# Opening of a one-core two-block transformer kernel: who issues the norm row and the first input transfer, and when the input's quarters are turned and squared

## The reference, cut to what matters

```python
def rms_norm(x, w):
    xf = x.astype(jnp.float32)
    y = xf * lax.rsqrt(jnp.mean(xf * xf, axis=-1, keepdims=True) + EPS)
    return (y * w.astype(jnp.float32)).astype(x.dtype)
...
def mixer_block(u, w_in, lb, hg_norm_w, rel_bias, w_branch_a, w_branch_b, w_out):
    z = u @ w_in
    ...
    return merged @ w_out
...
    h = x
    h = h + mixer_block(rms_norm(h, norm_mix_w[l]), w_in[l], ...)
    u = rms_norm(h, norm_mlp_w[l])
    h = h + jnp.square(jax.nn.relu(u @ w_up[l])) @ w_down[l]
```

## Time and profile before

| what | before |
|---|---|
| median of 3 runs | 1920.42 us (1920.09 to 1922.02) |
| profiled execution, its own time | 1919.19 us |
| its span | 1917.4 us |
| TensorE matmul, busy | 1889.7 us, 99% of the span |
| TensorE weight load, busy | 1752.5 us, 91% |
| VectorE, busy | 1101.7 us, 57% |
| ScalarE, busy | 914.2 us, 48% |
| GpSimd, busy | 178.9 us, 9% |
| mean traffic of the DMA engines | 181 GB/s |

### The profile page before, as it was taken

One profiled execution on the slowest core, in us unless ns is written; L12 is line 12 of the kernel. 1 busy time (PEld: TensorE's weight loads), 2 busy tenths in 40 slices (PEclk: granted clock), 3 DMA queues, 4 the chain that ended last, 5 costly groups with the idle time before them and its releaser, 6 DMA issues.

```text
span 1917.4 us, 33984 instructions
## 1 busy us (share of the span) xinstructions
PE 1889.7 (99%) x13468; PEld 1752.5 (91%) x13468; DVE 1101.7 (57%) x1265; ACT 914.2 (48%) x1189; POOL 178.9 (9%) x135
## 2 busy tenths in 40 slices
PE   9999999999999999999999999999999999998998
PEld 9989998999999889988998899899889998888986
DVE  6655766466655555554545545554566457766664
ACT  6534444565644455443443344344454354655543
POOL 2001331401000100000010000000010000031000
PEclk9999999999999999999999999999999999999999
DMA  8665656566565656666656666566555554444454
GB/s 272 191 180 171 185 179 177 152 193 177 171 220 186 208 187 177 196 199 189 196 187 198 190 195 194 190 183 202 188 185 173 175 170 133 116 136 144 133 187 143
DMA packets 176435, 346.49 MB, mean 181 GB/s; under 512 B 10976, under 2 KB 11184, under 8 KB 175776
## 3 DMA queue, kind: packets, MB, share of 16 engines
q1 hardware_dynamic: 174176, 337.76, 57.0%
q0 software_dynamic: 2128, 6.82, 1.4%
HBM read 342.44 MB, written 2.10 MB: 180 GB/s over the span
## 4 chain that ended last, share of the span: by engine, by line
PE 94%; DVE 3%; ACT 2%; issue 1%; DMA 0%; SPq 0%; POOL 0%; DVEq 0%; ACTq 0%
PE ps L430 56%; PE ps L442 32%; DVE wlo L1240 1%; ACT whi L857 1%; PE ps L758 1%; PE ps L527 1%; PE ps L745 1%; PE ps L722 0%; PE ps L460 0%; DMA x_nat<-in_x_dram 0%; PE ps L733 0%; PE ps L578 0%; PE ps L696 0%; DVE p L1652 0%; PE ps L570 0%
## 5 line engine op out<-in xcount | busy, mean ns | idle before, releaser
L1240 DVE TENSOR_TENSOR wlo<-raw,whi 128x1024 fp32r<-128x1024 f32 x631 | 804.1, 1280 | 719.3 <-ACT whi L857 718.3
L857 ACT ACTIVATE whi<-raw 128x1024 fp32r<-128x1024 f32 x631 | 664.1, 1058 | 872.6 <-PE ps L430 545.1
L430 PE MATMUL ps<-xhi,whi 128*128 128x256 f32 (+1 forms) x1984 | 567.3, 286 | 0.0
L430 PE MATMUL ps<-xhi,wlo 128*128 128x256 f32 (+1 forms) x1984 | 555.4, 280 | 0.0
L430 PE MATMUL ps<-xlo,whi 128*128 128x256 f32 (+1 forms) x1952 | 546.8, 280 | 0.0
L430 PEld LDWEIGHTS ps<-xhi,whi 128*128 128x128 f32 x1984 | 375.0, 189 | 10.0 <-issue 7.6
L430 PEld LDWEIGHTS ps<-xhi,wlo 128*128 128x128 f32 x1984 | 373.8, 188 | 0.0
L430 PEld LDWEIGHTS ps<-xlo,whi 128*128 128x128 f32 x1952 | 368.8, 189 | 1.5 <-issue 0.7
L430 PE MATMUL ps<-x2hi,whi 128*128 128x256 f32 x1024 | 282.8, 276 | 0.0
L430 PE MATMUL ps<-x2lo,whi 128*128 128x256 f32 x1024 | 282.7, 276 | 0.0
L430 PE MATMUL ps<-x2hi,wlo 128*128 128x256 f32 x1024 | 282.7, 276 | 0.0
(11 more groups left out here) (357 smaller groups left out, 2220.6 us busy)
## 6 DMA issues: line engine op xcount, KB each, us to landing
raw<-in_w_in_dram SPq DMA_DIRECT2D x279, 512.0 KB, 3.8
raw<-in_w_up_dram SPq DMA_DIRECT2D x128, 512.0 KB, 3.8
raw<-in_w_down_dram SPq DMA_DIRECT2D x128, 512.0 KB, 3.7
raw<-in_w_out_dram SPq DMA_DIRECT2D x64, 512.0 KB, 4.0
raw<-in_w_branch_a_dram SPq DMA_DIRECT2D x16, 512.0 KB, 4.2
raw<-in_w_branch_b_dram SPq DMA_DIRECT2D x16, 512.0 KB, 4.1
x_nat<-in_x_dram SPq DMA_DIRECT2D x4, 512.0 KB, 7.0
rel<-in_rel_turned_dram POOLq DMA_DIRECT2D x8, 256.0 KB, 4.4
```

The source lines that it names most:

```text
L430: ins = mm(outs[b], w[:, k % SLOTS, j, cols], v, start=start, stop=last and j == CK - 1 and i == 2, skip_group_check=True)
L857: f(whi[:, k % SLOTS], raw[:, k % SLOTS], ACT.Copy).then_inc(whi_ready, 1)
L1240: tt(wlo[:, k % SLOTS], raw[:, k % SLOTS], whi[:, k % SLOTS], ALU.subtract).then_inc(wlo_ready, 1)
```

## The change

- ScalarE issues the identity and `mix_rows`, ahead of its first table load; SyncE starts with the input at once.
- Quarter 0 of the input comes in two half transfers of 256 columns, the first (`x_first`) ahead of chunk 0's halves and the second (`x_in[0]`) behind them. Of chunks 1 to 3 and quarters 1 to 3 the chunk is issued first.
- TensorE waits for `x_first`, and within quarter 0 for `x_in[0]` ahead of row tile 2. Quarter c (1 to 3) is turned directly before chunk c, so one chunk later than before.
- The squares of quarter k are taken behind chunk 4 + k, by ScalarE and VectorE. The sum moves from behind chunk 4 to behind chunk 8, the square root from behind chunk 5 to behind chunk 8, reciprocal and `diag_m` from behind chunk 5 to behind chunk 9, the copy of `row_m` from behind chunk 10 to behind chunk 11.
- `row_scale()` stands before chunk 7 instead of chunk 6.

```diff
--- before.py
+++ after.py
@@ -244,6 +244,7 @@
         set_free = [sem(f"set_free{i}") for i in range(2)]
         kvb_free = [sem("kvb_free0"), sem("kvb_free1")]
         x_in = [sem(f"x_in{c}") for c in range(4)]
+        x_first = sem("x_first")
         half_in, half_hi, half_lo = [sem(n) for n in ("half_in", "half_hi", "half_lo")]
         ident_in, c_in, meta_in = [sem(n) for n in ("ident_in", "c_in", "meta_in")]
         vec_in, vec_t, vec_ready = sem("vec_in"), sem("vec_t"), sem("vec_ready")
@@ -358,17 +359,17 @@
             def rows(w, k, cols):
                 return w[:, CK * k:CK * k + CK, cols]
 
-            sp.dma_start(ident[:], identity).then_inc(ident_in, 16)
-            sp.dma_start(mix_rows[:], norm_mix_w[0].rearrange("(k p) -> k p", p=P)).then_inc(mix_in, 16)
-            for c in range(4):
-                cols = slice(c * CW, (c + 1) * CW)
-                sp.dma_start(x_nat[:, :, cols], x[0, :, cols].rearrange("(t p) d -> p t d", p=P)).then_inc(x_in[c], 16)
-                if c == 0:
-                    first = rows(w_in_t, 0, slice(0, CW))
-                    sp.dma_start(raw[:, 0, 0], first[:, 0]).then_inc(half_in, 16)
-                    sp.dma_start(raw[:, 0, 1], first[:, 1]).then_inc(raw_in[0], 16)
-                else:
-                    chunk(C_IN, c, rows(w_in_t, c, slice(0, CW)))
+            def x_cols(lo, hi):
+                return x_nat[:, :, lo:hi], x[0, :, lo:hi].rearrange("(t p) d -> p t d", p=P)
+
+            first = rows(w_in_t, 0, slice(0, CW))
+            sp.dma_start(*x_cols(0, CW // 2)).then_inc(x_first, 16)
+            sp.dma_start(raw[:, 0, 0], first[:, 0]).then_inc(half_in, 16)
+            sp.dma_start(raw[:, 0, 1], first[:, 1]).then_inc(raw_in[0], 16)
+            sp.dma_start(*x_cols(CW // 2, CW)).then_inc(x_in[0], 16)
+            for c in range(1, 4):
+                chunk(C_IN, c, rows(w_in_t, c, slice(0, CW)))
+                sp.dma_start(*x_cols(c * CW, (c + 1) * CW)).then_inc(x_in[c], 16)
             for k in range(4, NC):
                 chunk(C_IN, k, rows(w_in_t, k, slice(0, CW)))
             with sp.Fori(1, G_IN) as g:
@@ -464,10 +465,12 @@
 
             def turn_start(c):
 
-                pe.wait_ge(x_in[c], 16)
+                pe.wait_ge(x_in[c] if c else x_first, 16)
                 if c >= 2:
                     pe.wait_ge(x_ready, 4 * c - 4)
                 for kt in range(4 * c, 4 * c + 4):
+                    if kt == 2:
+                        pe.wait_ge(x_in[0], 16)
                     for t in range(NT):
                         o = (kt % 2) * T + t * P
                         ins = nc.tensor.transpose(ps[:, 4 + (kt % 8) // 2, o:o + P],
@@ -605,11 +608,11 @@
                             warm(11)
                             turn_start(0)
                             warm(9)
-                        if k < 3:
-                            turn_start(k + 1)
+                        if 1 <= k < 4:
+                            turn_start(k)
                         if k == 3:
                             turn_vectors()
-                        if k == 6:
+                        if k == 7:
                             row_scale()
                         pe.wait_ge(x_ready, CK * (k + 1))
                     if natural:
@@ -878,10 +881,14 @@
                 f(uhi[:, kt, :], ps[:, 4 + (kt % 8) // 2, (kt % 2) * T:(kt % 2) * T + T], ACT.Copy,
                   scale=mix_w[:, kt:kt + 1]).then_inc(n_hi, 1)
 
+            act.dma_start(ident[:], identity).then_inc(ident_in, 16)
+            act.dma_start(mix_rows[:], norm_mix_w[0].rearrange("(k p) -> k p", p=P)).then_inc(mix_in, 16)
             act.wait_ge(setup, 1)
             f(ss[:, 14:15], eps_t[:], ACT.Sqrt)
             def start_squares(c):
 
+                if c == 0:
+                    act.wait_ge(x_first, 16)
                 act.wait_ge(x_in[c], 16)
                 cols = slice(c * CW, (c + 1) * CW)
                 square(0, c, x_nat[:, 0, cols], junk[:, cols], 0, n_ss)
@@ -896,10 +903,8 @@
                         f(whi[:, 0, j], raw[:, 0, j], ACT.Copy).then_inc((half_hi, whi_ready)[j], 1)
                 else:
                     split_hi(C_IN, k)
-                    start_squares(k - 1)
             for kt in range(12, KT):
                 start_upper(kt)
-            start_squares(3)
 
             def start_meta():
                 act.wait_ge(meta_in, 16)
@@ -988,7 +993,9 @@
             for g in range(G_IN):
                 for k in range(NC):
                     split_hi(C_IN + NC * g, LEAD + k)
-                    if g == 0 and k == 1:
+                    if g == 0 and k < 4:
+                        start_squares(k)
+                    if g == 0 and k == 4:
                         act.wait_ge(n_sum, 1)
                         f(ss[:, 0:2], ss[:, 0:2], ACT.Sqrt, bias=eps_t[:], scale=1.0 / D).then_inc(n_sd, 1)
                     if g == 0 and k == 5:
@@ -1258,6 +1265,8 @@
             own(nc.vector.memset(ones[:], 1.0))
             def start_squares(c):
 
+                if c == 0:
+                    dve.wait_ge(x_first, 16)
                 dve.wait_ge(x_in[c], 16)
                 cols = slice(c * CW, (c + 1) * CW)
                 nc.vector.tensor_tensor_reduce(junk_b[:, cols], x_nat[:, 1, cols], x_nat[:, 1, cols], 1.0, 0.0,
@@ -1275,17 +1284,17 @@
                         tt(wlo[:, 0, j], raw[:, 0, j], whi[:, 0, j], ALU.subtract).then_inc((half_lo, wlo_ready)[j], 1)
                 else:
                     split_lo(C_IN, k)
-                    start_squares(k - 1)
             for kt in range(12, KT):
                 start_lower(kt)
-            start_squares(3)
 
             def start_rows(k):
 
-                if k == 0:
+                if k < 4:
+                    start_squares(k)
+                if k == 4:
                     dve.wait_ge(n_ss, 8)
                     nc.vector.tensor_reduce(ss[:, 0:2], sq[:, 0], AX.X, ALU.add).then_inc(n_sum, 1)
-                if k == 1:
+                if k == 5:
                     dve.wait_ge(n_sd, 1)
                     nc.vector.reciprocal(rstd[:, 0:2], ss[:, 0:2]).then_inc(n_rs, 1)
                     dve.wait_ge(n_rs, 1)
```

## The result

| | before | after |
|---|---|---|
| median of 20 runs each | 1919.36 us (1917.02 to 1923.62) | 1923.94 us (1921.53 to 1925.95) |
| ratio after / before | | 1.0020, 95% interval 1.0013 to 1.0027 |
| profiled execution's span | 1917.4 us | 1920.9 us |
| start of chunk 0 | 10.23 | 10.80 |
| start of chunk 4 | 23.70 | 25.58 |

The change makes the kernel slower, by some 4.6 us between the medians and by 2.5 to 5.2 us by the interval. The median lies in the range given and near the forecast of 1923.2, partly by luck: with 20 runs the kernel before came out at 1919.36 instead of 1920.42, so the rise is 4.6 us where I had summed up 2.8. Two misses offset each other: chunk 0, forecast 0.6 us earlier, came 0.57 later, and the kernel before was itself 1.1 us faster than I had taken it.

A forecast was written before the change was run, and what follows sets the result against it. TensorE was taken to bound the kernel (94% of the span), so its standstills in the first 40 us count. Terms -0.6 + 0.8 + 0.7 + 1.85 = 2.75 us put the median at 1923.2 us, range 1920.8 to 1925.8.

The forecast's parts named there:

- Identity and norm row: Opening: issued by ScalarE beside SyncE's input transfer, they land 0.2 us later, bounds 0 to 1.0 us.
- a start misjudged: Sign set beforehand for the opening: the start is misjudged if the warm-up doesn't begin within 0.5 us of 3.1.
- Start of chunk 0: Opening: turning starts at 5.93 instead of 6.15, chunk 0 near 9.65 instead of 10.23; gain 0.6 us.
- Quarter 1 behind chunk 0: Between chunks 0 and 1: quarter 1's 8 transposes now stand on TensorE's path; costs 0.8 us.
- Chunks 2 to 4: Quarters turned a chunk later: chunks 2 and 3 lose 0.1 us, chunk 4 waits 0.8 instead of 0.2; costs 0.7 us.
- The row scale: Before chunk 7: TensorE waits for the diagonals, which come after the moved squares, root and splits; costs 1.85 us.
- W: The end of `wlo` of chunk 4, from which the prediction counts times up to the row scale.
- What costs nothing: ScalarE's delayed table load, new `x_first` waits, later `row_m` copy and GpSimd's later small loads: no cost.
- The sum: Whole kernel: -0.6 + 0.8 + 0.7 + 1.85 = 2.75 us more, median 1923.2 us.
- (a): Rival: the clock falls in the new stop before `row_scale()`, 1.7 us more, 1924.9 us; chance 0.28.
- (b): Rival: identity and norm row land late, up to 1 us more at chunk 0, 1924.0 us; chance 0.08.
- (c): Rival: no stop before `row_scale()`, chunk 4 waits as before; 1920.6, possibly 1920.0 us; chance 0.12.

The follow-up runs named there:

- the first two experiments: Changed kernel with identity and norm row issued by SyncE again, span 1923.7 us; changed kernel with SyncE's input waiting for both to land, span 1922.4 us.

## Why the prediction was right or wrong

- **Identity and norm row.** This step failed. "I take 0.2 us, since its own bytes are few, and keep 0 to 1.0": it was 1.5 us (the warm-up starts at 4.66 for 3.12), outside the bounds that I kept and, by the prediction's own sign (within 0.5 us of 3.1), a start misjudged. The mechanism was named, a transfer beside the input's; the size was not. The worst case that I thought through, waiting until the whole 256 KB are through, is what happens, and it had been priced too low.
- **Start of chunk 0.** "Gain 0.6 us" was a loss of 0.57. The norm row is the cause in the changed kernel, where the lower part of chunk 0 is split 0.9 us later than before (9.97 for 9.11). With SyncE's issues that part is through by 9.2, and then the late second half, which the prediction had waved through ("may cost a few tenths") and which is waited for 1.31 us, together with slow warm-ups, holds chunk 0 at 10.68. What the order of the transfers costs or gives alone, in the kernel before, no run shows. A small misreading besides: the 11 warm-ups' 2.61 us run to a modelled end, and the turning behind them starts 2.4 us after their first (4.66 to 7.07), 0.2 us sooner than the prediction's sum has it.
- **Quarter 1 behind chunk 0.** Right in kind; the two kernels with later squares, without and with later turning, differ by 1.4 us at chunk 4, and my two terms for it (0.8 and 0.7) add up to 1.5.
- **Chunks 2 to 4.** Predicted waits 0.1 and 0.8, measured about 0.1 and, in starts, 0.75; the term was 0.7 and 0.6 came. The statement that the squares' move shortens this is shown: 1.20 us of waiting with them, 0.58 without, by the brackets.
- **The row scale.** Right in size and in working. The prediction had the diagonals at W + 10.45 and TensorE at W + 8.75. Chunk 4's `wlo` ended at 25.43 (24.20 and 1.23), the diagonals at 35.88, so at W + 10.45, and TensorE stood there by 34.1, W + 8.7. Predicted 1.85 us, in starts 1.8 and 2.1. Taking the row scale out of the way returned it.
- **What costs nothing.** Up to group 4 no wait of TensorE goes back to anything on this list.
- **The sum.** 2.75 predicted, 3.8 at chunk 7. Chunk 0's start is 1.2 us of difference (0.57 later instead of 0.6 earlier), and the other terms together came out 0.1 us below their sum.
- **Rivals.** (a) is real: the clock fell behind the row scale in one of two executions of the changed kernel, and behind the stop of 4.66 us. It didn't fall behind stops of 1.94 and 1.95 us in the first two experiments, and behind 2.04 to 2.05 us in the attention it fell in eight of thirteen, so my point from which it decides, around 2 us, is a region and no edge. The prediction read one fall at 2.05 us as a rule. How often it falls behind the row scale can't be told from these runs; its share may make the median's rise (4.6) larger than that of the first executions' spans (3.5), but this is not shown. (b) came true in every kernel that issued the norm row beside the input, and its time, 1924.0, is the one measured; that the two agree to 0.1 us is luck, since the kernel before came out 1.1 us faster. Its chance, 0.08, rested on "few bytes", which the landings refute. (c) is out. The ratio sits on the bound of 0.2% and doesn't decide between no change and slower.
- The Trainium skill's rule (DMA: Bandwidth & Descriptors, Issuing engines are not separate DMA queues) fits what the runs show in one point: ScalarE's queue alone was no quicker than SyncE's, 1.6 us for the norm row on both. That the transfers "interleave" is no promise for a small one: issued beside an input transfer of 256 or of 512 KB, it landed behind the input both times.

## What to carry to other kernels

A small transfer on which everything waits belongs ahead of the bulk, not beside it on another queue; check its landing, not its issue. In the kernel before it stood there, and moving it alone cost 1.5 us at chunk 0; in the changed kernel putting it back gained only 0.1 us, since the next wait took over. When a chain of side work is moved behind later steps, move its reader by the length of the chain, not by one step: count what the slower engine has to do in between, and where the reader can wait until the end of a group, put it there. Work taken off the wait before the first step and put behind it is no longer hidden: in this kernel it cost 1.7 us from chunk 0 to chunk 4, for 0.2 us of an earlier start.

## What the runs showed of the hardware that I had not expected

- A norm row of 8 KB on ScalarE's queue landed 0.1 to 0.3 us behind the input transfer issued before it on SyncE's queue, with 256 KB (3.1 us after its issue) and with 512 KB (4.3 us), and in 1.6 us when nothing was beside it.
- The same matmuls follow each other at 0.113 or 0.118 us with the granted clock at 1.00 (47 or 45 in 5 us; 91 or 87 in 10 us), over stretches of 20 us and more. It differs between executions of one kernel, and changes at interruptions of the stream but also within it (in the changed kernel at 19.2 us, inside chunk 2). What sets it stays open; over 20 us it is worth a us, as much as most terms here.
- The clock's falls are not tied to the kernel: behind the same stop of 2.04 to 2.05 us in the attention it fell to between 0.57 and 0.70 on the mean of 4 us in eight of thirteen executions, and stayed at 1.00 in five, among them one of two of the same kernel. Behind the row scale a fall cost 1.5 us (stop of 1.95 us) and 1.6 us (4.66 us).
- At the start the distance of the transposes varies with no fall in the clock column: the 9 warm-ups took 1.15 us in the changed kernel, 1.47 us in its second execution, and 2.13 us in the kernel with the row scale behind chunk 7, whose opening is the same, and the granted clock of the windows there is 1.00 in all three.
